# Two-block model on one core: the feed forward's single pair of inner rows moves from the first group of the product back to the last

## The chip, the cores and the metric

One core of a Trainium2 chip runs one program. The metric is the device time of that core in microseconds (us); less is better. The time before is the median of three runs.

## The reference, cut to what matters

Two models run one after the other on a sequence of 256 tokens with width 1024: a first block (two layers with three branches each), then a second block (two layers, each a mixing part and a feed forward). The second block also carries a context of 256 tokens. Its feed forward is what the change touches:

```python
D_FF = 2816
def conv_ffn(h, w_up, conv_w, w_down):
    a = dwconv_centred(h @ w_up, conv_w)      # three taps along the tokens
    val, gate = jnp.split(a, 2, axis=-1)
    return (val * jax.nn.silu(gate)) @ w_down

x = x + g2 * conv_ffn(hf, w_up[l], conv_w[l], w_down[l])
if not last:                                  # layer 0 does the context too
    xc = xc + cg2 * conv_ffn(hcf, w_up[l], conv_w[l], w_down[l])
```

In layer 0 both streams go through, 512 columns wide; in layer 1 only the 256 tokens. Behind it stands a root mean square norm with a scale and a shift that come from a conditioning vector (`c`, `c_ctx`) through `w_mod`.

## The kernel before, in words

Activations lie with their channels on the partitions: `t_X` holds 8 tiles of 128 channels by two streams of 256 tokens, all in float32. To keep that precision, every weight and every activation is split into a high and a low part, and each product is three matmuls: high by high, high by low, low by high (L1003, L1004, L1005 in `chan`).

**Weights.** They arrive in rows of 128 by 1024 floats, loaded by SP's queue into 8 raw buffers. A `split` step turns a row into a high part on ScalarE (L1410) and then a low part on VectorE (L1740). There are 5 slots (`NS`) for split chunks. The split of chunk i + 5 waits until TensorE has used chunk i for the last time (`used`), and it stands in the order of ScalarE and VectorE where the planner put it.

**The order.** One planner (`Order`) writes a single list of steps. Each engine goes through this list in order and does its own part of each step, with semaphore waits in between. `gemm` plans one product: it takes chunks of weights, cuts the output into parts that each take one of four PSUM banks (`gb0` to `gb3`, reused in turn), puts the split of the chunk five ahead of its first one before the last part, and that of its second chunk, if it has one, behind. `tick` lets generators in `self.side` add one step each (gated products, sums of squares). An `urgent` product (the last of a stage) cuts its last parts finer, ticks between the parts and leaves the splits of its own chunks to the norm behind it (`late`, `high_first`, `lows`, `late_splits`). `mod_turn` puts a conditioning step (`mod`, matmuls L1095) after every third product of the feed forward in layer 0, as long as more than 6 of them are left; its bank is emptied by `modsum` on VectorE (L1801) or, for every fourth one, on ScalarE (L1456).

**The feed forward of layer 0** (`block2(0)`). The 2816 inner rows are 22 tiles, handled as 11 pairs. For each pair there are two up products, value (`vg` = 0) and gate (`vg` = 1), each 8 tiles deep with 256 output rows: 48 matmuls of 512 columns. Behind each part ScalarE applies the middle tap (L1700) and VectorE the side taps (L2185, twice). `glu` follows one product later: SiLU on ScalarE (L1710), product on VectorE (L2200), high part on ScalarE (L1712), low part on VectorE (L2202), into `Y2` and `YL2`, which hold two groups of four tiles. The product back, `down(g)`, reads one group and comes in two halves of 512 output rows. Each half has four parts (m = 0 to 3), one bank each, and its two x updates per part are L2158 on VectorE. The groups are: pair 0 alone (two tiles), then pairs 1 and 2, 3 and 4, 5 and 6, 7 and 8, 9 and 10 (four tiles each). A half with two tiles takes one chunk of weights, a half with four tiles takes two.

`down(5)` ends the feed forward. Before it, the generator of the squares is put in `self.side`: squares of x tiles 0 to 3 behind the first half, 4, 5, 6 and 7 one by one behind the parts of the second half, which is urgent (`down`, c = 11). A square is L1436 on ScalarE and its sum L1765 on VectorE. Then the norm: TensorE's sum over the partitions in two steps (L1077, which waits for the sum with tile 6, and L1068), conditioning steps between them, the root on ScalarE, the reciprocal on VectorE, its spread over the partitions (L1084), the normalised tiles on VectorE and ScalarE (`norm2`), and then the `wide` product of layer 1, whose tiles are taken as the norm hands them over.

The lines that the steps speak of: the group of a pair is `g, p2 = (pr + 1) // 2, (pr + 1) % 2`, written out in `block2`, in `glu` on ScalarE and VectorE and in `ffup` on both. In `down` of TensorE, `yv` is the first slot of the group in `Y2`. The order of the up and down products:

```python
for vg in range(len(first), 2):
    self.gemm("up", ...)
if p2 == 1 and g >= 1:
    self.need_mods(l, 5)
    down(g - 1)
```

Of the kernel before, what the change touches and what calls it, by code (L numbers as in the profile page):

```python
# [66 lines left out]
class Marks:  # L67
# [17 lines left out]
    def at(self, *event):  # L85
        return self.table[event] if self.sems else {}
# [76 lines left out]
class Order:  # L163
# [427 lines left out]
    def block2(self, l):  # L591
        last = l == L - 1
        tw = 256 if last else 512
        nz = tw // 256
        t = 3 + 2 * l
        self.every = 0 if last else 3
        if last:
            self.need_mods(l, 1)
            self.add("s1", l=l, x=(1, t))
            b = self.rstd(t, (1, 1, 1))  # L600
            self.add("norm2", l=t, g=b, x=range(8))
            self.behind_sums()
            self.late_splits()
            self.wide(l, [("uf", c, wcols("w_in_2", l, 768 + np.arange(c * 256, c * 256 + 256)), 256, lambda m: (0, 1), None)
                          for c in range(2)], 256, t)
        else:
            self.between()
        self.side.append(self.mixes(l, nz))
        self.fine = True
        i = self.chunk(CH, wcols("w_in_2", l, np.concatenate([BY_HALF, 64 + BY_HALF, 128 + np.arange(128)])))  # L610
        self.add("k2", l=l, i=i, g=(self.bank(),))
        self.rope2_then(l, "k", 0)
        self.tick()
        self.split_after(i, 0)
        self.add("v2", l=l, i=i, g=(self.bank(),))
        self.side.append(self.v2_turn(l))
        self.split_after(i, 1)
        self.tick()
        for c in range(2):
            self.gemm("q2", l, c, wcols("w_in_2", l, 256 + LAT_PERM.reshape(8, 64)[4 * c:4 * c + 4, BY_HALF].reshape(256)), 8, 256, tw,  # L620
                      then=lambda m0: [self.rope2_then(l, "q", 2 * c + m) for m in range(m0, min(2, m0 + 512 // tw))] and ())
        self.drain()
        units = [(z, m, qb) for z in range(nz) for m in range(4) for qb in range(2)]
        self.side.append(self.staggered([self.pair(l, n, *u) for n, u in enumerate(units)], range(len(units))))
        for bi, nkt, wn, perm in ((1, 2, "w_br_pool_2", None), (2, 2, "w_br_four_2", None), (0, 4, "w_br_attn_2", LAT_PERM)):
            for c in range(4):
                self.gemm("gate2", l, c, wcols("w_in_2", l, 1280 + bi * 1024 + np.arange(c * 256, c * 256 + 256)), 8, 256,
                          tw, x=(bi, tw))
                if bi == 0 and c == 0:
                    self.drain()  # L630
                if bi == 0 and c == 3:
                    for k in range(6):
                        self.add("msplit2", l=l, c=k)
                self.gemm("proj2", l, c, wcols(wn, l, np.arange(c * 256, c * 256 + 256), perm), nkt, 256, tw,
                          x=(bi, tw, nkt, len(units)))
        self.fine = False
        for k in (6, 7):
            self.add("msplit2", l=l, c=k)
        self.tick()
        self.need_mods(l, 2)  # L640
        self.every = 0
        self.side.append(self.squares(t + 1, PAIRED))
        def wout2(c):
            return wcols("w_out_2", l, np.arange(c * 256, c * 256 + 256))
        first = (0, 1) if last else (0,)
        self.wide(l, [("wout2", c, wout2(c), 256, lambda m: (m, min(2, m + 512 // tw)), None) for c in first], tw, -1)
        for c in first:
            self.tick()
            self.mod_turn()
        for c in range(len(first), 4):  # L650
            self.gemm("wout2", l, c, wout2(c), 8, 256, tw, urgent=c == 3, early=last, soon=c == 2)
        self.drain()
        self.need_mods(l, 4)
        self.add("s1", l=l, x=(4, t + 1))
        b = self.rstd(t + 1, (1, 1, 1 if last else 2))
        self.add("norm2", l=t + 1, g=b, x=range(8))
        self.behind_sums()
        self.late_splits()
        self.every, self.keep = 0 if last else 3, 6

        def down(g):
            nt = 4 if g else 2
            for half in range(2):
                self.gemm("down", l, 2 * g + half, wcols("w_down_2", l, np.arange(half * 512, half * 512 + 512),
                                                         max(0, 4 * g - 2) * 128 + np.arange(nt * 128)), nt, 512, tw,
                          urgent=g == 5 and half == 1, early=not last, x=(nt,))
        for pr in range(11):
            g, p2 = (pr + 1) // 2, (pr + 1) % 2
            first = () if pr else range(512 // tw if last else 1)
            if pr == 0:  # L670
                self.wide(l, [("up", 0, wcols("w_up_2", l, vg * DFF + np.arange(256)), 256,
                               lambda m, vg=vg: (m, min(2, m + 512 // tw), vg),
                               lambda m, vg=vg: self.up_then(l, 0, vg, m, tw)) for vg in first], tw, t + 1)
                self.tick()
                self.mod_turn()
            for vg in range(len(first), 2):
                self.gemm("up", l, pr, wcols("w_up_2", l, vg * DFF + np.arange(pr * 256, pr * 256 + 256)), 8, 256, tw,
                          x=(vg,), then=lambda m0: self.up_then(l, pr, vg, m0, tw))
            if p2 == 1 and g >= 1:
                self.need_mods(l, 5)  # L680
                down(g - 1)
                if not last and g == 3:
                    self.add("c3", l=1)
        self.drain()
        self.side.append(self.squares(t + 2, ((0, 1, 2, 3), (4, 5), (6,), (7,)) if last else ((0, 1, 2, 3), (4,), (5,), (6,), (7,))))
        down(5)
        self.drain()
        self.every = 0
# [204 lines left out]


IDLE = {0: (11, 2, 5), 1: (0, 0, 1), 4: (0, 0, 1), 5: (0, 0, 3), 6: (0, 0, 2)}


def blocks_of(s):
# [68 lines left out]
def tensor(e, units, t, M):  # L967
# [53 lines left out]
    def idle(b, t_, part):  # L1021

        src = t.C32.rearrange("p k c -> p (k c)") if t_ == 0 and part == 0 else t.C1
        for _ in range(IDLE.get(t_, (0, 0, 0))[part]):
            mm(b[:, 0:256], src[:, 0:128], src[:, 0:256], start=True, stop=True)
# [327 lines left out]

    def down(u):
        tw, g, nt = 256 if u.l else 512, u.c // 2, u.x[2]
        yv = (g % 2) * 4 + 4 - nt
        chan(u, nt, 512, tw, lambda k: t.Y2[:, yv + k, 0:tw], lambda k: t.YL2[:, yv + k, 0:tw],
             lambda k: at("glu", u.l, g, yv + k), ("downmm", u.l, g))

# [27 lines left out]
def scalar(e, units, t, M):  # L1387
# [305 lines left out]

    def ffup(u):
        l, pr, vg, tw = u.l, u.c, u.x[2], 256 if u.l else 512
        D, p2 = (t.VT, t.GT)[vg], (pr + 1) % 2
        b = gbank(u)
        for j, m in enumerate(range(u.x[0], u.x[1])):
            q.wait_ge(was("fr", l, vg, pr - 2, m), at("m2", l))
            act(D[:, p2, m, 0:tw], b[:, j * tw:(j + 1) * tw], ACT.Copy,  # L1700
                scale=vec("conv2", (l * 3 + 1) * 44 + vg * 22 + 2 * pr + m)).then_inc(*up("act", ("upa", l, pr, vg, m)))

    def glu(u):
        l, pr, tw = u.l, u.c, 256 if u.l else 512
        g, p2 = (pr + 1) // 2, (pr + 1) % 2
        for m in range(u.x[0], u.x[1]):
            yi = (g % 2) * 4 + 2 * p2 + m
            G, V = t.GT[:, p2, m, 0:tw], t.VT[:, p2, m, 0:tw]
            q.wait_ge(at("upd", l, pr, 1, m))
            act(G, G, ACT.Silu).then_inc(*up("act", ("glus", l, pr, m)))  # L1710
            q.wait_ge(at("gluv", l, pr, m), was("downmm", l, g - 2), at("wout2mm", l))
            act(t.Y2[:, yi, 0:tw], V, ACT.Copy).then_inc(*up("act", ("gluh", l, pr, m), ("glu", l, g, yi), ("fr", l, 0, pr, m)))  # L1712
# [10 lines left out]
def vector(e, units, t, M):  # L1723
    q, up, at, was, last = Queue(e, M), M.up, M.at, M.was, lambda: M.last("dve")
# [449 lines left out]

    def ffup(u):
        l, pr, vg, tw = u.l, u.c, u.x[2], 256 if u.l else 512
        D, p2, b = (t.VT, t.GT)[vg], (pr + 1) % 2, t.gb[u.g[0] % 4]
        ms = list(enumerate(range(u.x[0], u.x[1])))

        def side(j, m, w):  # L2180
# [11 lines left out]

    def glu(u):
        l, pr, tw = u.l, u.c, 256 if u.l else 512
        g, p2 = (pr + 1) // 2, (pr + 1) % 2
        for m in range(u.x[0], u.x[1]):
            yi = (g % 2) * 4 + 2 * p2 + m
            G, V = t.GT[:, p2, m, 0:tw], t.VT[:, p2, m, 0:tw]
# [259 lines left out]
```

## Time and profile before

| What | Value |
|---|---|
| Median of 3 runs | 2054.66 us (2052.29 to 2056.34) |
| Profiled execution, its own time | 2052.45 us |
| Its span, first to last instruction | 2050.7 us |
| TensorE busy | 2030.4 us, 99% |
| VectorE busy | 1361.2 us, 66% |
| ScalarE busy | 1100.1 us, 54% |
| GpSimd busy | 71.3 us, 3% |
| Mean granted TensorE clock | 0.998 |
| Feed forward of layer 0 | about 1280 to 1650 us of the span |

The busy time of TensorE is modelled from pipelined matmuls: a record of 0.39 us stands every 0.23 us, so records overlap, and the distance of two starts tells the pace. An idle time is shown in brackets in front of the instruction that ended it, with the instruction that released it.

### The profile page before, as it was taken

What the parts mean: (1) busy time and instruction counts of PE and PEld (TensorE: products, weight loads), DVE (VectorE), ACT (ScalarE), POOL (GpSimd) and SP (SyncE); (2) the same over time, 40 slices, a digit from 0 to 9 for tenths busy, and PEclk for the clock granted to TensorE, in tenths of its full rate; (3) what the DMA queues carried; (4) which work ended last, traced back from release to release, by engine and by line L of the source; (5) the groups of instructions that cost most, each with busy time, mean ns of one, the idle gap of its engine ahead of it and who ended that gap; (6) DMA issues with size and microseconds to landing.
All of it is one profiled execution on the core that took longest, in us unless ns stands there. A gap on an engine that the chain in (4) does not pass through costs nothing.

```text
span 2050.7 us, 36323 instructions
## 1 busy us (share of the span) xinstructions
PE 2030.4 (99%) x14736; PEld 1822.3 (89%) x14736; DVE 1361.2 (66%) x2349; ACT 1100.1 (54%) x1839; POOL 71.3 (3%) x55
## 2 busy tenths in 40 slices
PE   9999999999999999999999999999999999999998
PEld 9999999999999999998777887778888878999998
DVE  6787767557687777574565345665555667668786
ACT  5576676545676685553575233433332357655554
POOL 1310000000300000000000000000000000000000
PEclk9999999999999999999999999999999999999999
DMA  8546645567656635563223434433343344456552
GB/s 296 184 159 215 191 145 166 194 210 253 225 171 198 205 124 190 201 206 134 90 73 114 144 134 144 145 114 131 113 159 123 104 154 131 147 178 217 186 181 67
DMA packets 97351, 333.97 MB, mean 163 GB/s; under 512 B 11552, under 2 KB 16160, under 8 KB 96928
## 3 DMA queue, kind: packets, MB, share of 16 engines
q1 hardware_dynamic: 97184, 331.64, 47.8%
q8 instruction: 117, 1.92, 0.4%
q14 instruction: 50, 0.41, 0.1%
HBM read 326.49 MB, written 1.18 MB: 160 GB/s over the span
## 4 chain that ended last, share of the span: by engine, by line
PE 92%; DVE 4%; ACT 2%; issue 1%; DMA 0%; DVEq 0%; SPq 0%; ACTq 0%
PE ps L1003 26%; PE ps L1004 25%; PE ps L1005 25%; PE ps L1095 2%; PE ps L1016 2%; PE ps L1017 1%; PE ps L1018 1%; PE ps L1315 1%; PE ps L1168 1%; DVE t_lo L1740 1%; PE ps L1336 1%; PE ps L1325 1%; PE ps L1184 1%; ACT t_hi L1410 1%; PE ps L1149 1%
## 5 line engine op out<-in xcount | busy, mean ns | idle before, releaser
L1003 PE MATMUL ps<-t_RB,t_hi 128*128 128x256 f32 (+1 forms) x3712 | 1160.2, 313 | 3.8 <-DVE t_MT L1801 2.2
L1004 PE MATMUL ps<-t_RB,t_hi 128*128 128x256 f32 (+1 forms) x3712 | 1144.0, 308 | 0.0
L1005 PE MATMUL ps<-t_RB,t_lo 128*128 128x256 f32 (+1 forms) x3712 | 1143.7, 308 | 0.0
L1740 DVE TENSOR_TENSOR t_lo<-t_raw,t_hi 128x1024 fp32r<-128x1024 f32 (+1 forms) x500 | 604.7, 1225 | 357.7 <-ACT t_hi L1410 356.2
L1003 PEld LDWEIGHTS ps<-t_RB,t_hi 128*128 128x128 f32 x3712 | 707.9, 191 | 72.4 <-issue 22.7
L1005 PEld LDWEIGHTS ps<-t_RB,t_lo 128*128 128x128 f32 x3712 | 708.1, 191 | 35.3
L1004 PEld LDWEIGHTS ps<-t_RB,t_hi 128*128 128x128 f32 x3712 | 708.4, 191 | 33.0
L1410 ACT ACTIVATE t_hi<-t_raw 128x1024 fp32r<-128x1024 f32 (+1 forms) x506 | 519.4, 1041 | 376.4 <-PE ps L1005 353.5
L2185 DVE SCALAR_TENSOR_TENSOR t_A<-ps,t_V,t_A 128x510 f32<-128x510 f32 (+1 forms) x176 | 102.1, 611 | 89.7 <-ACT t_A L1700 88.1
L1700 ACT ACTIVATE t_A<-ps,t_V 128x512 f32<-128x512 f32 (+1 forms) x88 | 48.4, 576 | 127.2 <-PE ps L1005 127.2
L2158 DVE SCALAR_TENSOR_TENSOR t_X<-ps,t_MOD,t_X 128x256 f32<-128x256 f32 x168 | 72.5, 477 | 33.1 <-PE ps L1005 33.1
L1016 PE MATMUL ps<-t_hi,t_RB 128*128 128x256 f32 x256 | 74.8, 292 | 0.0
L1017 PE MATMUL ps<-t_hi,t_RB 128*128 128x256 f32 x256 | 73.0, 285 | 0.0
L1018 PE MATMUL ps<-t_lo,t_RB 128*128 128x256 f32 x256 | 73.0, 285 | 0.0
L1686 ACT ACTIVATE t_A<-ps 128x512 f32<-128x512 f32 (+1 forms) x48 | 22.3, 490 | 84.3 <-PE ps L1005 84.3
L1712 ACT ACTIVATE t_RB<-t_A 128x512 fp32r<-128x512 f32 (+1 forms) x44 | 23.1, 526 | 57.5 <-DVE t_A L2200 57.5
L1016 PEld LDWEIGHTS ps<-t_hi,t_RB 128*128 128x128 f32 x256 | 49.7, 194 | 1.5 <-DVE t_RB L2047 0.5
L1095 PE MATMUL ps<-t_raw,t_C 128*32 128x256 f32 x768 | 51.0, 385 | 0.0
L1017 PEld LDWEIGHTS ps<-t_hi,t_RB 128*128 128x128 f32 x256 | 49.8, 195 | 0.0
L1018 PEld LDWEIGHTS ps<-t_lo,t_RB 128*128 128x128 f32 x256 | 49.7, 194 | 0.0
L1436 ACT ACTIVATE t_NT<-t_X 128x256 f32<-128x256 f32 (+1 forms) x56 | 24.8, 467 | 37.5 <-DVE t_X L2158 21.6
L1966 DVE SCALAR_TENSOR_TENSOR t_A<-ps,t_V,t_A 128x255 f32<-128x255 f32 (+2 forms) x96 | 41.7, 475 | 1.1
(307 smaller groups left out, 1846.2 us busy)
## 6 DMA issues: line engine op xcount, KB each, us to landing
t_raw<-in_W SPq DMA_DIRECT2D x586, 512.0 KB, 4.0
t_A<-cu_scratch SPq DMA_DIRECT2D x8, 512.0 KB, 6.1
t_B<-cu_scratch SPq DMA_DIRECT2D x8, 512.0 KB, 6.1
t_raw<-in_W SPq DMA_DIRECT2D x16, 256.0 KB, 2.8
t_A<-t_T SPq DMA_DIRECT2D x40, 64.0 KB, 4.5
t_A<-in_C SPq DMA_DIRECT2D x2, 1280.0 KB, 7.2
t_A<-t_T SPq DMA_DIRECT2D x40, 32.0 KB, 1.9
t_X<-in_X SPq DMA_DIRECT2D x2, 512.0 KB, 4.4
```

The source lines that it names most:

```text
L1003: mm(o, hi[:, w], xh(k), start=k == 0 and j == 0, stop=False)
L1004: mm(o, hi[:, w], xl(k), start=False, stop=False)
L1005: i = mm(o, lo[:, w], xh(k), start=False, stop=k == nkt - 1 and m == u.x[1] - 1)
L1016: mm(o, xh(k, tb), hi[:, w], start=k == 0 and j == 0, stop=False)
L1017: mm(o, xl(k, tb), hi[:, w], start=False, stop=False)
L1018: i = mm(o, xh(k, tb), lo[:, w], start=False, stop=k == nkt - 1 and tb == blocks[-1])
L1095: i = mm(b[32 * c:32 * c + 32, 0:256], t.C32[:, k, :], t.raw[r % NR][:, c * 256:c * 256 + 256], start=u.s[0] and h == 0, stop=u.s[1] and h ...
L1410: act(t.hi[s][:, 0:w], t.raw[r][:, 0:w], ACT.Copy).then_inc(*up("act", ("hi", u.i), ("split", u.i)))
L1700: act(D[:, p2, m, 0:tw], b[:, j * tw:(j + 1) * tw], ACT.Copy, scale=vec("conv2", (l * 3 + 1) * 44 + vg * 22 + 2 * pr + m)).then_inc(*up("a ...
L1740: tt(t.lo[s][:, 0:w], t.raw[r][:, 0:w], t.hi[s][:, 0:w].bitcast(F), ALU.subtract).then_inc(*up("dve", ("split", u.i)))
L2158: stt(out=x, in0=ps[:, z * 256:z * 256 + 256], scalar=t.modv(u.l, j, k, z), in1=x, op0=ALU.mult, op1=ALU.add).then_inc(*up("dve", ("x", s, ...
L2185: return stt(out=o[:, :, r], in0=ps[:, :, s], scalar=cw, in1=o[:, :, r], op0=ALU.mult, op1=ALU.add)
```

## The change

In layer 0 the pairs are grouped 0 and 1, 2 and 3, and so on to 8 and 9, and pair 10 is a group by itself. So the group with two tiles is the last one of the product back instead of the first. Layer 1 keeps the grouping that both had. A function `pair_of(l, pr)` gives group and place of a pair for both layers: `divmod(pr + l, 2)`. The products back of layer 0 then follow up 3, 5, 7, 9 and 10 (before: 2, 4, 6, 8 and 10), and `down(5)` comes last as before. The load of the constants `c3` follows `down(2)` in both.

```diff
         def down(g):
-            nt = 4 if g else 2
+            nt = 2 if g == (0 if last else 5) else 4
             for half in range(2):
                 self.gemm("down", l, 2 * g + half, wcols("w_down_2", l, np.arange(half * 512, half * 512 + 512),
-                                                         max(0, 4 * g - 2) * 128 + np.arange(nt * 128)), nt, 512, tw,
+                                                         (max(0, 4 * g - 2) if last else 4 * g) * 128 + np.arange(nt * 128)), nt, 512, tw,
                           urgent=g == 5 and half == 1, early=not last, x=(nt,))
         for pr in range(11):
-            g, p2 = (pr + 1) // 2, (pr + 1) % 2
+            g, p2 = pair_of(l, pr)
...
-            if p2 == 1 and g >= 1:
+            if (p2 == 1 or pr == 10) and g >= 1:
                 self.need_mods(l, 5)
                 down(g - 1)
...
+def pair_of(l, pr):
+
+    return divmod(pr + l, 2)
...
     def down(u):
         tw, g, nt = 256 if u.l else 512, u.c // 2, u.x[2]
-        yv = (g % 2) * 4 + 4 - nt
+        yv = (g % 2) * 4 + (4 - nt if g == 0 else 0)
...
     def ffup(u):
         l, pr, vg, tw = u.l, u.c, u.x[2], 256 if u.l else 512
-        D, p2 = (t.VT, t.GT)[vg], (pr + 1) % 2
+        D, p2 = (t.VT, t.GT)[vg], pair_of(l, pr)[1]
...
     def glu(u):
         l, pr, tw = u.l, u.c, 256 if u.l else 512
-        g, p2 = (pr + 1) // 2, (pr + 1) % 2
+        g, p2 = pair_of(l, pr)
```

`ffup` and `glu` change in the same way on ScalarE and on VectorE.

## Rows read from the trace of the kernel before

**Rows 1.** The page: the engines' busy time, the chain that ended last.
```profile
PE 2030.4 (99%) x14736; PEld 1822.3 (89%) x14736; DVE 1361.2 (66%) x2349; ACT 1100.1 (54%) x1839; POOL 71.3 (3%) x55
PE 92%; DVE 4%; ACT 2%; issue 1%; DMA 0%; DVEq 0%; SPq 0%; ACTq 0%
```

**Rows 2.** Waits of PE, 1250 to 1720 us: total us, times, longest; both that there are.
```profile
PE ps L1003 <- DVE t_MT L1801: 2.2, 1, 2.2
PE ps L1077 <- DVE t_SQA L1765: 1.2, 1, 1.2
```

**Rows 3.** Timeline of PE in the first product back: start us, duration us, instruction, [idle].
```profile
1353.30 0.39 PE L1005 MATMUL ps<-t_RB,t_lo 128*128 128x512 f32 x1
1355.91 0.50 PE L1003 MATMUL ps<-t_RB,t_hi 128*128 128x512 f32 x1 [2.22 <-DVE t_MT L1801]
```

**Rows 4.** Timeline of DVE at the same place.
```profile
1351.46 0.68 DVE L2200 TENSOR_TENSOR t_A<-t_A 128x512 f32<-128x512 f32 x1
...
1355.44 0.41 DVE L1801 TENSOR_TENSOR t_MT<-t_MT,ps 128x256 f32<-128x256 f32 x1
1355.77 2.44 DVE L2158 SCALAR_TENSOR_TENSOR t_X<-ps,t_MOD,t_X 128x256 f32<-128x256 f32 x6
```

**Rows 5.** Timeline of PE: ends of down 5's halves, and the norm behind.
```profile
1638.52 0.39 PE L1005 MATMUL ps<-t_RB,t_lo 128*128 128x512 f32 x1
...
1649.39 0.39 PE L1005 MATMUL ps<-t_RB,t_lo 128*128 128x512 f32 x1
1650.95 1.02 PE L1077 MATMUL ps<-t_C,t_SQA 128*128 128x1 f32 x8 [1.17 <-DVE t_SQA L1765]
...
1654.89 0.65 PE L1084 MATMUL ps<-t_C,t_SM 128*128 128x128 f32 x4
```

**Rows 6.** Timeline of DVE in down 5.
```profile
1636.22 0.88 DVE L2158 SCALAR_TENSOR_TENSOR t_X<-ps,t_MOD,t_X 128x256 f32<-128x256 f32 x2 [1.84 <-PE ps L1005]
1638.73 1.23 DVE L1740 TENSOR_TENSOR t_lo<-t_raw,t_hi 128x1024 fp32r<-128x1024 f32 x1 [1.63 <-ACT t_hi L1410]
1639.88 0.87 DVE L2158 SCALAR_TENSOR_TENSOR t_X<-ps,t_MOD,t_X 128x256 f32<-128x256 f32 x2
1640.66 2.27 DVE L1765 TENSOR_TENSOR t_SQA<-t_SQA,t_NT 128x512 f32<-128x512 f32 x3
1642.99 1.23 DVE L1740 TENSOR_TENSOR t_lo<-t_raw,t_hi 128x1024 fp32r<-128x1024 f32 x1
1644.13 0.87 DVE L2158 SCALAR_TENSOR_TENSOR t_X<-ps,t_MOD,t_X 128x256 f32<-128x256 f32 x2
...
1646.37 0.87 DVE L2158 SCALAR_TENSOR_TENSOR t_X<-ps,t_MOD,t_X 128x256 f32<-128x256 f32 x2
```

**Rows 7.** Timeline of ACT: the high part in the first half of down 5.
```profile
1637.64 1.06 ACT L1410 ACTIVATE t_hi<-t_raw 128x1024 fp32r<-128x1024 f32 x1 [8.46 <-PE ps L1005]
```

**Rows 8.** Windows: stretch, us, busy us (x) of PE to POOL, PEclk, DMA share, GB/s.
```profile
921.00:924.00 3.00, 1.85 (x24) 1.39 (x24) 1.02 (x4) 1.49 (x4) 0.00 (x0) 1.00 0.12 49
924.00:928.00 4.00, 4.00 (x24) 3.89 (x21) 3.57 (x9) 1.93 (x4) 0.00 (x0) 0.57 0.72 262
...
1638.90:1650.00 11.10, 10.88 (x49) 8.67 (x47) 8.80 (x15) 6.24 (x11) 0.00 (x0) 1.00 0.28 94
...
1654.00:1657.00 3.00, 3.00 (x38) 1.62 (x37) 2.02 (x6) 1.17 (x4) 0.00 (x0) 1.00 1.00 340
```

**Rows 9.** Timeline of PE around 924 us, where the second block begins.
```profile
918.06 0.28 PE L1018 MATMUL ps<-t_lo,t_RB 128*128 128x256 f32 x1
918.18 0.28 PE L1016 MATMUL ps<-t_hi,t_RB 128*128 128x256 f32 x1
...
922.15 0.58 PE L1077 MATMUL ps<-t_C,t_SQA 128*128 128x1 f32 x4 [1.29 <-DVE t_SQA L1765]
...
925.02 0.41 PE L1016 MATMUL ps<-t_hi,t_RB 128*128 128x256 f32 x1
925.24 0.41 PE L1017 MATMUL ps<-t_hi,t_RB 128*128 128x256 f32 x1
```

More of the change, by code:

```diff
@@ L2176, in ffup @@
         l, pr, vg, tw = u.l, u.c, u.x[2], 256 if u.l else 512
-        D, p2, b = (t.VT, t.GT)[vg], (pr + 1) % 2, t.gb[u.g[0] % 4]
+        D, p2, b = (t.VT, t.GT)[vg], pair_of(l, pr)[1], t.gb[u.g[0] % 4]
         ms = list(enumerate(range(u.x[0], u.x[1])))
@@ L2194, in glu @@
         l, pr, tw = u.l, u.c, 256 if u.l else 512
-        g, p2 = (pr + 1) // 2, (pr + 1) % 2
+        g, p2 = pair_of(l, pr)
         for m in range(u.x[0], u.x[1]):
```

## The prediction

> **What bounds the kernel now.** The page comes first. TensorE is busy for 99% of the span and the chain that ended last lies on it for 92% [rows 1], so the change can only act where TensorE stands still, or where it runs at another clock. The work of the product is the same in both kernels: 22 up products, and 22 tiles of inner rows for the product back, however they are grouped. So the next view is the list of TensorE's own waits in the stretch of this feed forward (1250 to 1720 us). It holds two entries: 2.2 us, once, for the sum L1801 into t_MT, and 1.2 us, once, for the sum of squares L1765 [rows 2]. The first lies at the small group that now stands at the start, the second right behind the last group. Both are touched by the change, in opposite directions.
>
> The profiled execution took 2052.45 us (span 2050.7, the rest lies around it). The median of the three runs is 2054.66, 2.2 above it. My sum is a difference, worked out in the profiled execution and added to the median.
>
> **The start stall goes: -2.4 us.** Matmuls of 512 columns follow each other every 0.2265 us (48 matmuls from 1638.52 to 1649.39 [rows 5]). A quarter (one m) of a half of down has 3 matmuls per tile: 12 with four tiles, 2.72 us, and 6 with two tiles, 1.36 us. In the small group at the start, down c=1 takes its fourth bank back from the conditioning matmuls issued between its two halves. That bank is freed by the VectorE sum L1801, which is queued behind the two gated products of pair 2 (1351.46 to 1355.4) [rows 4]. TensorE gets to the point after three quarters of 1.36 us and stops: it issues at 1353.30 and next at 1355.91, where 1353.53 was due: 2.38 lost [rows 3]. After the change the first group has four tiles, and counting the chunks' products (one conditioning step per three) its step comes behind up 3's value half, followed by the gate half (48 matmuls, 10.9 us) before the bank comes round again. L1801 is 4 us late at most, so 10.9 us cover it. The next step comes behind down c=1, again before an up product. Value -2.4; bounds 0 (another bank takes its place) and -2.6 (with the slow first matmuls after the stall).
>
> **Order inside the body: 0.** Every down product has the same two up products between it and the last gated product that it reads, except the last pairs. Down 4 reads pair 9, with down 3's second half and up 10 in between (over 30 us); down 5 reads pair 10, with the 21.7 us of down 4 (96 matmuls) in between, as now. The buffers Y2/YL2 are freed one product before they are written, as now. If that cover were gone, a wait for a gated product would cost about the 4 us of its chain [rows 4]. The c3 load and the weight loads keep their order in SP's queue. c3 is issued one pair (about 22 us) later, but its reader is in the next layer; 0. The conditioning steps are as many as before. Split steps: as many, but one moves from behind the norm to before it (below).
>
> **The end: +5.7 us.** This is the term that decides. Call E0 the end of the first half of down 5 (1638.91: last issue 1638.52 plus 0.39) and E the end of its last matmul (1649.78) [rows 5]. Between them TensorE now has 10.87 us of work; with two tiles it has 5.44.
> VectorE's work there does not shrink. Now [rows 6]: low part of a chunk at 1638.73, the fourth x update at 1639.88 (E0+0.97), three sums of squares from 1640.66 (2.33 until the next), a low part at 1642.99 (1.14), the first x update of the last half at 1644.13. From there each quarter is a chain of x update, square on ScalarE and sum on VectorE, 2.2 us each (1644.13, 1646.37), whatever TensorE does. TensorE's sum over partitions starts when the seventh sum is done, at 1650.95, 6.82 behind that first update: E0+12.04, E+1.17.
> After: the low part of the chunk five ahead sits before the fourth x update in VectorE's order. The slot that it needs is now freed by the very last matmul of the half, since the chunk is the whole half, instead of by its sixth (1637.54, ScalarE's high part at 1637.64 [rows 7]). So the high part starts at E0+0.10, the low part at E0+1.19, the update at E0+2.34 (+1.15), the sums at E0+3.12 (+0.78), and the first update of the last half at E0+5.45 (+2.33; the second low part is gone, which saves 1.14). TensorE starts again at E0+5.45+6.82 = E0+12.27. But E is now E0+5.44. The gap is 6.83 instead of 1.17: +5.66.
> VectorE has idle time in the first half (1.84 before 1636.22 [rows 6]), but its next work there waits for TensorE, so none of it can be drawn ahead. Bounds: with no backlog at all the four-quarter chain alone, started at E-4.08, ends at E+2.8: +1.7; with a low part more in front, +6.8. I take 5.66, since each step has its own row. Nothing hides it: the conditioning matmuls put there to fill the norm stand behind the waiting instruction in TensorE's queue.
> Behind the norm one low part fewer waits. TensorE stood still for none there [rows 2], so that is 0.
>
> **The clock: +2.5 us.** The kernel's granted clock fell to half (1.2 of 2.4 GHz) only once before its end: at 924.3, after 1.29 us without work and thin work behind it (922.15 on) [rows 8, 9]. The distance of two matmuls went from 0.12 (918.06, 918.18) to 0.21 (925.02, 925.24). The 4 us from 924 have a mean clock of 0.57, so some 3.4 us ran at half, which cost 1.5. At the end of this feed forward, a gap of 1.17 left it at 1.00 [rows 5, 8]. A gap of 6.8 has no row; it is five times the one that was followed by a fall, so I take it that it falls. What follows the gap is a chain on TensorE: sum over partitions, conditioning step, second sum, conditioning step, spread of the root, 1650.95 to 1655.5, 4.5 us [rows 5]. At half clock it is longer by 0.78 (0.2133 against 0.12): 3.5 if the whole chain runs so, 1.5 if only as long a stretch does as at 924. Value 2.5. Bounds: 0, and 4.8 with some 1.3 more in the first steps of the wide product, which go at VectorE's pace.
> The Trainium skill (TensorE: Matmul & The Clock Gate, the part on the HAM clock gate) says that an idle stretch puts the engine back to 1.2 GHz and that only sustained work brings it back. It speaks against this change: by it the fall is certain and the sum +5.8. By the gap that left the clock at 1.00 alone, the sum would be +3.3. The trace agrees that the clock can fall within the kernel, not yet how surely.
>
> **Sum.** -2.38 + 5.66 + 2.5 = +5.8: the profiled execution would come to 2058.2, the median to 2060.4. A measurement of this kernel tells about 0.2% (4.1 us) from no change.
>
> **The rivals.**
> (a) The clock holds. For: 1.17 us did nothing. Against: the gap is almost six times that. -2.4 + 5.7 = +3.3: 2058.0, within 0.2%. Chance 0.15.
> (b) The other side: VectorE keeps up, and only the start stall's removal is left. Place: first update of the last half. For: there is room, since VectorE is busy for 8.8 of 11.1 us of the last half as it is [rows 8], and a low part leaves its queue. The change comes out not slower if the gap behind E is under 1.17 + 2.4 = 3.6 us, that is if that update starts by E0+2.2 instead of E0+5.45. Against: low part, update and three sums, 4.3 us, stand before it in order. Full case: 2052.3; at its border 2054.7. Chance 0.12.
> (c) The start stall returns at another bank or gated product: +8.2, 2062.8. Against: products of 10.9 us instead of 5.4 everywhere. Chance 0.08.
> (d) The clock stays low through the chain and into the wide product, since thin work does not raise it: -2.4 + 5.7 + 4.8 = +8.1: 2062.7. For: thin work at 921 to 924 was followed by the fall [rows 8]. Chance 0.14.
> (e) The change does nothing, since the group sizes are the same set: 2054.7; it would need both gaps unchanged. Chance 0.02.
> My forecast has the remaining 0.49.
>
> **How the numbers follow.** The likeliest is 2060.4. Its own spread is about 2 either way (clock term 1.5 to 3.5, median of a few runs about 1). The range takes in (a), (c), (d) and the forecast: 2056.2 to 2064.4, and leaves out (b), (e) and tails. Slower by over 0.2% (above 2058.8): most of the forecast (0.42) and (c), (d): 0.64. Within 0.2%: (a), (e), most of (b) (0.10) and the low part of the forecast (0.07): 0.34. Faster by over 0.2% (below 2050.6) needs more than the 3.6 us of both stalls together, so it is left with 0.02 out of (b).
>
> **What would show it.** In the profile after: no wait of L1003 for L1801 near 1354; TensorE idle 6 to 7 us before L1077 at some 1648 to 1654, released by L1765; 24 matmuls of L1003 to L1005 between the two halves' ends; the x update, square, sum rhythm of 2.2 us unchanged; a clock under 1.00 in the windows behind the gap, matmul records there longer by about three quarters; the later stages shifted as a whole. It is wrong if the gap is under 3.6 us, or if a new wait shows in the body.

## The result, and the profile after

The changed kernel takes 2058.70 us in the median of 16 runs (2057.72 to 2059.68). The kernel before, in 16 runs beside it and before it, takes 2055.97 (2052.29 to 2057.52). The ratio is 1.0019, with a 95% interval of 1.0012 to 1.0025: slower by 2.5 to 5.1 us, just inside the 0.2% that the prediction had set as its line. The predicted median was 2060.4 in a range of 2056.2 to 2064.4, with 0.64 on slower by over 0.2%, which did not come, and 0.34 on a difference within it.

The profiled execution took 2058.21 us with a span of 2056.4; the prediction had 2058.2 for it.

| | before | after |
|---|---|---|
| Median, 16 runs each | 2055.97 us | 2058.70 us |
| Profiled execution / span | 2052.45 / 2050.7 us | 2058.21 / 2056.4 us |
| Mean granted clock of it | 0.998 | 0.995 |
| TensorE's waits, 1250 to 1720 us | 2.2 and 1.2 us | 6.7 us |
| From the sum over partitions to the spread of the root | 4.6 us | 8.4 us |

The page after, the lines that answer to [rows 1] (busy time; chain that ended last):

```profile
PE 2033.1 (99%) x14736; PEld 1823.9 (89%) x14736; DVE 1360.7 (66%) x2349; ACT 1100.7 (54%) x1839; POOL 71.4 (3%) x55
...
PE 93%; DVE 4%; ACT 2%; issue 1%; DVEq 0%; ACTq 0%
```

As many matmuls as before, and the busy share still reads 99%. These two lines would not lead anyone to the cause. The list of PE's waits from 1250 to 1720 us does. It has one entry (lines have moved by 5; L1082 is the sum over the partitions, L1770 the sum of squares):

```profile
PE ps L1082 <- DVE t_SQA L1770: 6.7, 1, 6.7
```

The start wait of [rows 2] is gone and the one at the end has grown from 1.2 to 6.7 us. PE's timeline there, to be held beside [rows 5]:

```profile
1640.10 0.39 PE L1010 MATMUL ps<-t_RB,t_lo 128*128 128x512 f32 x1
...
1645.54 0.39 PE L1010 MATMUL ps<-t_RB,t_lo 128*128 128x512 f32 x1
1652.62 1.84 PE L1082 MATMUL ps<-t_C,t_SQA 128*128 128x1 f32 x8 [6.68 <-DVE t_SQA L1770]
1654.38 1.93 PE L1100 MATMUL ps<-t_raw,t_C 128*32 128x256 f32 x16
1656.24 1.87 PE L1073 MATMUL ps<-t_C,t_NT 128*128 128x1 f32 x8
1658.04 1.93 PE L1100 MATMUL ps<-t_raw,t_C 128*32 128x256 f32 x16
1659.91 1.12 PE L1089 MATMUL ps<-t_C,t_SM 128*128 128x128 f32 x4
```

1640.10 is the last matmul of the first half, 1645.54 that of the second, 24 matmuls later. Behind the gap every record takes 1.7 to 1.8 times as long as in [rows 5]: 1.84 for 1.02 us, 1.12 for 0.65. The windows show why (columns as in [rows 8]):

```profile
924.00:928.00 4.00, 4.00 (x40) 3.75 (x33) 3.42 (x9) 1.93 (x4) 0.00 (x0) 1.00 0.74 262
1646.00:1652.00 6.00, 0.00 (x0) 0.00 (x0) 3.85 (x9) 3.62 (x6) 0.00 (x0) 0.77 0.00 0
1652.00:1656.00 4.00, 3.38 (x24) 2.37 (x24) 2.65 (x6) 1.32 (x2) 0.00 (x0) 0.50 0.12 16
1656.00:1662.00 6.00, 6.00 (x44) 3.68 (x44) 1.54 (x5) 0.69 (x3) 0.00 (x0) 0.50 0.91 336
1662.00:1666.00 4.00, 4.00 (x33) 3.04 (x23) 4.00 (x11) 2.68 (x8) 0.00 (x0) 0.89 0.89 329
```

The clock falls within the gap and stays at half (1.2 of 2.4 GHz) through the whole thin chain, until the wide product is about to begin. At 924, where the profiled execution before had lost 1.5 us, the clock holds this time. VectorE's and ScalarE's timelines for the same place, beside [rows 6, 7]:

```profile
1640.59 1.06 ACT L1415 ACTIVATE t_hi<-t_raw 128x1024 fp32r<-128x1024 f32 x1 [4.38 <-PE ps L1010]
```

```profile
1641.68 1.23 DVE L1745 TENSOR_TENSOR t_lo<-t_raw,t_hi 128x1024 fp32r<-128x1024 f32 x1 [1.31 <-ACT t_hi L1415]
1642.82 0.87 DVE L2163 SCALAR_TENSOR_TENSOR t_X<-ps,t_MOD,t_X 128x256 f32<-128x256 f32 x2
1643.61 2.28 DVE L1770 TENSOR_TENSOR t_SQA<-t_SQA,t_NT 128x512 f32<-128x512 f32 x3
1645.80 0.87 DVE L2163 SCALAR_TENSOR_TENSOR t_X<-ps,t_MOD,t_X 128x256 f32<-128x256 f32 x2
1647.43 0.69 DVE L1770 TENSOR_TENSOR t_SQA<-t_SQA,t_NT 128x512 f32<-128x512 f32 x1 [0.76 <-ACT t_NT L1441]
1648.04 0.87 DVE L2163 SCALAR_TENSOR_TENSOR t_X<-ps,t_MOD,t_X 128x256 f32<-128x256 f32 x2
```

When the first update of the last half starts (1645.80), TensorE has already issued that half's last matmul (1645.54).

Where 5.5 of the 5.8 us between the two profiled executions come from: the last matmul of down 5 ends at 1645.93 instead of 1649.78 (-3.85: the start stall of 2.4, and the fall at 924 that is absent here, 1.5). The gap is 6.68 instead of 1.17 (+5.51). From its end to the end of the spread it takes 8.41 instead of 4.59 (+3.82). Together +5.48; the first matmul behind the wide product starts at 1676.06 instead of 1670.58, also 5.48 later. The wide product itself starts 5.96 later (1664.04 instead of 1658.08): the half clock also cost 0.5 us in the steps between the spread and the wide product, and the wide product made that up.

### The profile page after: what moved, and what is told of

Same layout as the page of the kernel before. It is cut to its first block, busy times and chain, and to the rows that moved or that the text cites. A ratio compares the mean times of both kernels' runs of the same rounds, so it can differ in the third digit from the quotient of the medians.

```text
span 2056.4 us, 36322 instructions
## 1 busy us (share of the span) xinstructions
PE 2033.1 (99%) x14736; PEld 1823.9 (89%) x14736; DVE 1360.7 (66%) x2349; ACT 1100.7 (54%) x1839; POOL 71.4 (3%) x55
## 4 chain that ended last, share of the span: by engine, by line
PE 93%; DVE 4%; ACT 2%; issue 1%; DVEq 0%; ACTq 0%
PE ps L1008 26%; PE ps L1009 25%; PE ps L1010 25%; PE ps L1100 2%; PE ps L1021 1%; PE ps L1022 1%; PE ps L1023 1%; PE ps L1320 1%; PE ps L1173 1%; DVE t_lo L1745 1%; PE ps L1341 1%; PE ps L1330 1%; PE ps L1189 1%; PE ps L1154 1%; PE ps L1030 1%
```

## The experiments

Theory T is the prediction's: two gaps of TensorE, both made by VectorE's queue, and the clock behind the one at the end. Theory U: the clock falls in any case in the thin work of the norm (its small matmuls, of one column or on 32 columns of weights), and the gap hardly matters. Theory V: the regrouping costs time in the body of the loop. Each ratio is to the kernel before on the same chip, with its 95% interval. In diffs, `A` stands for the changed kernel as base and `B` for the kernel before.

| Kernel | Median us (runs) | Kernel before beside it | Ratio | Span of its profile |
|---|---|---|---|---|
| mid_pair | 2054.04 (12) | 2055.38 | 0.9996 (0.9988 to 1.0005) | 2049.3 |
| before_turn | 2055.87 (12) | 2055.38 | 1.0001 (0.9993 to 1.0010) | 2054.2 |
| before_fill | 2053.05 (12) | 2055.38 | 0.9993 (0.9984 to 1.0001) | 2052.7 |
| after_fill | 2059.62 (11) | 2055.38 | 1.0018 (1.0010 to 1.0027) | 2056.3 |
| after_fill13 | 2055.49 (11) | 2054.51 | 1.0005 (0.9996 to 1.0014) | 2053.6 |
| after_late | 2055.81 (11) | 2054.51 | 1.0009 (1.0000 to 1.0018) | 2056.0 |
| before_glu | 2051.09 (11) | 2054.51 | 0.9987 (0.9978 to 0.9996) | 2050.7 |
| glu_pipe | 2047.08 (5) | 2054.51 | 0.9967 (0.9954 to 0.9979) | 2045.2 |
| after_pipe | 2057.54 (11) | 2056.16 | 1.0010 (1.0001 to 1.0019) | 2055.8 |
| before_pipe | 2052.36 (11) | 2056.16 | 0.9984 (0.9975 to 0.9993) | 2050.6 |
| after_all | 2051.11 (11) | 2056.16 | 0.9977 (0.9968 to 0.9986) | 2049.7 |
| glu_pipe_fill | 2049.51 (6) | 2056.16 | 0.9969 (0.9958 to 0.9981) | 2046.4 |

### The start: which part of the small group makes the wait

**mid_pair**: pair 4 alone, so that first and last group both have four tiles.

```diff
 def pair_of(l, pr):
-    return divmod(pr + l, 2)
+    return divmod(pr + (l or pr > 4), 2)
...
-            nt = 2 if g == (0 if last else 5) else 4
+            nt = 2 if g == (0 if last else 2) else 4
-            if (p2 == 1 or pr == 10) and g >= 1:
+            if (p2 == 1 or (pr == 4 and not last)) and g >= 1:
```

The row offset follows, and `VT`, `GT` go by `pr % 2`.

> The pair of two tiles stands in the middle (pair 4 is a group by itself), so both the first and the last group have four tiles. Theory T (two gaps): the start wait of 2.2 us is gone, the gap behind down 5 is back at 1.2 us, the chain of the norm takes 4.6 us at full clock in most executions; profiled span 2048.3 (2050.7 less 2.4), median 2 to 3 us under the kernel before and 4 to 8 us under the changed one. Theory V (the regrouping itself costs time in the body of the loop): a wait of 1 us or more shows somewhere between 1290 and 1630, and the time is not under that of the kernel before.

The end came out as T had it: the gap is 1.17 us again. The start did not: T had the wait gone. It has moved with the small group (PE's timeline):

```profile
1490.33 0.50 PE L1008 MATMUL ps<-t_RB,t_hi 128*128 128x512 f32 x1 [2.22 <-DVE t_MT L1806]
```

It is as long as in [rows 3] and stands at down 2, now the small one. The span of 2049.3 is 1.4 under the kernel before because the clock held at 924 in this execution; the ratio shows no difference from 1, where T had the median 2 to 3 us lower. Theory V falls as well: the list of waits from 1250 to 1720 has these two entries and no other.

**before_turn**: the conditioning steps moved by one product, so that none stands between the halves of the small group.

```diff
         self.every, self.keep = 0 if last else 3, 6
+        self.turn += 0 if last else 1
```

> The kernel before with the conditioning steps of this feed forward moved by one product, so that none stands between the halves of the small group. Groups as before. Theory T: only the start wait goes, 2.2 to 2.4 us less (span 2048.3), the gap at the end stays at 1.2. If the wait at the start was the small group's own (shorter parts against VectorE's queue, whoever holds the bank), a wait of 1 to 2 us stays there and the gain is under 1 us.

The second case came true, with a longer wait than the 1 to 2 us expected. It has another releaser, the x update instead of the conditioning sum:

```profile
1355.23 0.50 PE L1004 MATMUL ps<-t_RB,t_hi 128*128 128x512 f32 x1 [2.58 <-DVE t_X L2159]
```

So the bank's holder was not the cause. VectorE is busy with the two gated products from 1350.33 to 1354.3 here too, and whatever frees a bank stands behind them.

This profile shows something else that the prediction had at nothing. Right behind the stall the clock falls. The windows there (columns as in [rows 8]), before_turn first, then before_fill (see below; its stall is 2.22 us, as in [rows 3]), then the kernel before:

```profile
1356.00:1360.00 4.00, 4.00 (x12) 3.09 (x11) 2.66 (x5) 0.00 (x0) 0.00 (x0) 0.58 0.28 81
```

```profile
1356.00:1360.00 4.00, 4.00 (x11) 3.15 (x12) 2.56 (x7) 1.06 (x1) 0.00 (x0) 0.57 0.06 23
```

```profile
1356.00:1360.00 4.00, 4.00 (x18) 3.29 (x19) 3.45 (x8) 1.06 (x1) 0.00 (x0) 1.00 0.08 28
```

While it is down the 512-column matmuls start 0.43 us apart instead of 0.23, and the fall costs 1.6 us each time. It shows in three of the five profiles that have such a stall (before_turn, before_fill, before_pipe; not in the kernel before nor in mid_pair) and in none of the nine that have no such stall, the changed kernel's among them. So where the clock falls the start stall costs 4.0 us and not 2.4.

**before_glu**: the gated product of pair 2 one product later, the conditioning step where it was.

```diff
-    def later(self, kind, **k):
+    def later(self, kind, more=0, **k):
         def g():
             yield
+            for _ in range(more):
+                yield
...
-            self.later("glu", l=l, c=pr, x=
+            self.later("glu", more=int(l == 0 and pr == 2), l=l, c=pr, x=
```

> The kernel before with the gated product of pair 2 one product later, behind the second half of the small group instead of between its halves. The conditioning step stays between the halves. mid_pair and before_turn have shown that the start wait follows the small group whoever holds the bank; theory T now says that it is the 4 us of gated product in VectorE's queue ahead of the first half's last x update. Expected: no wait at 1354, 2.2 to 2.4 less; span 2048.3 where the clock holds, median 2 us under the kernel before. If the small group's parts are too short for VectorE even without it, a wait of 0.5 us or more stays.

The wait is gone; only the end's is left in the list of PE's waits, and the conditioning sum (now L1803) runs at 1352.16 instead of 1355.44 ([rows 4]), right behind the x update:

```profile
1351.38 0.87 DVE L2160 SCALAR_TENSOR_TENSOR t_X<-ps,t_MOD,t_X 128x256 f32<-128x256 f32 x2
1352.16 0.41 DVE L1803 TENSOR_TENSOR t_MT<-t_MT,ps 128x256 f32<-128x256 f32 x1
```

The ratio of 0.9987 (2.7 us, interval 0.8 to 4.5) agrees with 2.4 us, and with some more. In its profile the sum over the partitions starts 1.82 us earlier than in [rows 5] (1649.13 against 1650.95); the execution was already 0.7 us late at 922. One thing stays open: T had 2048.3 for the span of an execution in which the clock holds, and none of the 11 came to that (the lowest took 2050.50, the mean clock was 0.996 or 0.997 in all). So the start stall is made by short parts and the gated products together: 5.4 us of matmuls per half against 4 us of VectorE that nothing may pass.

### The clock behind the last group

**after_fill** and **after_fill13** (A), **before_fill** (B): matmuls without use in TensorE's queue ahead of the sum over the partitions, 24, 13 and 4 of them. `u.l == 5` is the norm behind this feed forward.

```diff
     def rstda(u):
...
         b = bank(u)
+        for _ in range(13 if u.l == 5 else 0):
+            mm(b[:, 0:256], t.C1[:, 0:128], t.C1[:, 0:256], start=True, stop=True)
         q.wait_ge(at("sqadd", u.l, 6))
```

> The changed kernel with 24 matmuls of 256 columns (float32, 0.26 us each, 6.3 us) that compute nothing of use, in TensorE's queue between the last matmul of down 5 and the sum over the partitions. They add no wait: the sum's wait for L1770 still ends last. Theory T: the gap of 6.7 is filled, the clock stays at 1.00, the chain from the sum to the spread of the root takes 4.6 us instead of 8.4; span 2052.6 or so, 3.5 to 4 us under the changed kernel. Theory U (the clock falls by itself in the thin work of the norm, gap or no gap): the clock still shows under 1 behind 1652 and the time stays within 1 us of the changed kernel. If the gap is not VectorE's doing, the fillers push the sum back and the time rises by up to 6 us.

The price per filler was wrong: each leaves two records, 0.22 us apart, so 24 took 10.6 us and pushed the sum back by 4.2 us (1656.86 instead of 1652.62). That mistake makes it a clean measurement of the clock. PE's timeline:

```profile
1646.40 10.63 PE L1081 MATMUL ps<-t_C 128*128 128x256 f32 x48 [0.79 <-DVE t_X L2165]
1656.86 0.95 PE L1084 MATMUL ps<-t_C,t_SQA 128*128 128x1 f32 x8
...
1660.72 0.65 PE L1091 MATMUL ps<-t_C,t_SM 128*128 128x128 f32 x4
```

The chain starts 4.24 us later than in the changed kernel and ends at 1661.37, only 0.34 later, since it runs at full clock: 4.51 us against 8.41. The spans are 2056.3 and 2056.4.

> As after_fill, but 13 matmuls instead of 24: after_fill's record shows two passes of 0.22 us for each, so 24 took 10.6 us and outlasted the gap, while the chain behind them ran at full clock in 4.5 us. 13 take 5.7 us and end with the gap. Theory T: the sum starts when the seventh sum of squares is done, as in the changed kernel, the chain takes 4.6 us instead of 8.4: span 2052.6, median 3 to 4 us under the changed kernel's 2058.7, that is within 1.5 us of the kernel before. Theory U: clock under 1 there all the same, time as the changed kernel's.

```profile
1647.99 5.88 PE L1081 MATMUL ps<-t_C 128*128 128x256 f32 x26 [0.79 <-DVE t_X L2165]
1653.79 1.05 PE L1084 MATMUL ps<-t_C,t_SQA 128*128 128x1 f32 x8
...
1657.75 0.65 PE L1091 MATMUL ps<-t_C,t_SM 128*128 128x128 f32 x4
```

Here the last matmul of down 5 ends at 1647.20 (1647.99 less 0.79; this execution had lost time at 924, as the kernel before did). 6.6 us later the sum starts, the stretch being as long as before but full except for the first 0.79 us, and 4.6 us after that the chain is through. The ratio goes from the changed kernel's 1.0019 to 1.0005, and the median from 2058.7 to 2055.5 (on different chips). That is about 3 us; T had 3 to 4, and the intervals of the ratios are too wide to tell more. Theory U falls: with the gap filled the clock holds through the thin chain. All 14 profiles, the kernels below included, bear this out. With the gap filled, gone, or 0.55 us long the clock held through the chain in seven of seven (after_fill, after_fill13, before_fill, after_all, before_pipe, glu_pipe, glu_pipe_fill). Behind 4.4 to 6.7 us it was at half in three of three (the changed kernel, after_late, after_pipe). Behind 1.17 us it held in two (the kernel before, mid_pair) and fell in two (before_turn, before_glu).

> The kernel before with 4 such matmuls (1.0 us) in its gap of 1.2 us. Theory T: same span as the kernel before when that one keeps its clock (2050.7); if the other executions of the kernel before (median 3.5 us above the profiled one) lose time by a fall of the clock behind this gap, the median falls by 1 to 3 us. Theory U: no change of the median, since the thin work behind is what counts.

The median beside its own kernel before is 2.3 us lower (2053.05 against 2055.38), as T had it, with an interval of the ratio that just includes 1. These fillers were too many as well: they took 1.7 us in a gap of 1.17 and pushed the sum back by 0.55 us. The clock held behind them in the profile. This fits the wider scatter of the kernel before, which the falls at 1356 add to. In the 90 executions of the kernel before that stand beside these experiments, 26 took under 2054 us, with a mean clock of 0.997 to 0.998; the others, up to 2058.9, show 0.994 to 0.997. The changed kernel always shows 0.994 to 0.996. before_glu's profile, with the kernel before's gap of 1.17, shows such an execution:

```profile
1649.13 1.02 PE L1079 MATMUL ps<-t_C,t_SQA 128*128 128x1 f32 x8 [1.17 <-DVE t_SQA L1767]
1650.08 1.07 PE L1097 MATMUL ps<-t_raw,t_C 128*32 128x256 f32 x16
1651.08 1.33 PE L1070 MATMUL ps<-t_C,t_NT 128*128 128x1 f32 x8
1652.34 1.93 PE L1097 MATMUL ps<-t_raw,t_C 128*32 128x256 f32 x16
1654.20 1.12 PE L1086 MATMUL ps<-t_C,t_SM 128*128 128x128 f32 x4
```

The clock falls in the middle of the chain (the third record is 1.33, the fourth 1.93 instead of 1.07). The end of the spread is at 1655.32, 0.2 us before that of [rows 5], although the chain began 1.8 us earlier.

### The end: what makes the gap

**after_late** (A): the split of the first half's chunk leaves the half and joins those behind the norm.

```diff
             if last and not urgent and hold:
+                self.late.append(i)
+            elif last and not urgent:
                 self.split_after(i, 0)
```

`hold` is set for the first half of down 5 in layer 0.

> The changed kernel, with the split of the chunk that the first half of down 5 frees moved out of the half (as the last half's already is): its high part comes behind the last part, its low part behind the sum over the partitions. Theory T (VectorE's queue sets the gap): the fourth x update starts at E0+0.1 to 0.2 instead of E0+2.3, so the gap shrinks by 2.2, from 6.7 to 4.5; the chain is at half clock as before; span 2 us under the changed kernel's. If the gap were the four-quarter chain's alone, it would stay at 6.7.

VectorE's fourth x update comes right behind TensorE, and the gap shrinks to 4.40 us, by 2.28:

```profile
1642.87 0.88 DVE L2165 SCALAR_TENSOR_TENSOR t_X<-ps,t_MOD,t_X 128x256 f32<-128x256 f32 x2 [0.15 <-PE ps L1012]
```

```profile
1652.67 0.56 PE L1084 MATMUL ps<-t_C,t_SQA 128*128 128x1 f32 x2 [4.40 <-DVE t_SQA L1772]
```

The gap is as expected. The span of its profile is not 2 us lower, since this execution was 0.8 us later at 922 already, then had a fall at 924 (1.5 us), and so came to the end of down 5 2.3 us later than the changed kernel's. The ratio, 1.0009 against 1.0019, agrees with 2 us, with overlapping intervals.

**after_pipe** (A), **before_pipe** (B), **glu_pipe** (before_glu and this edit): each sum of squares one part later, so that VectorE never waits for a square that ScalarE has only just begun.

```diff
-((0, 1, 2, 3), (4,), (5,), (6,), (7,))
+((0, 1, 2), (3,), (4,), (5, 6), (7,))
```

> The changed kernel with the sums of squares one part later in VectorE's order, as in glu_pipe. Theory T: the split ahead of the fourth x update stays, the chain of update, square, sum no longer costs 2.2 us a part; first update of the last half at E0+4.6 instead of 5.5, seventh sum done at E0+10.5: gap 5.0 instead of 6.7, clock still half behind it, span and median 1.5 to 2 us under the changed kernel. If the gap were set by the amount of VectorE's work alone and not by the order, it would stay at 6.7.

The gap is 5.09 us. The parts are now 1.4 us apart on VectorE (1646.48 and 1647.87 instead of 2.2 apart), about what TensorE needs for one part of the short half (1.36):

```profile
1646.48 0.87 DVE L2163 SCALAR_TENSOR_TENSOR t_X<-ps,t_MOD,t_X 128x256 f32<-128x256 f32 x2
1647.27 0.68 DVE L1770 TENSOR_TENSOR t_SQA<-t_SQA,t_NT 128x512 f32<-128x512 f32 x1
1647.87 0.87 DVE L2163 SCALAR_TENSOR_TENSOR t_X<-ps,t_MOD,t_X 128x256 f32<-128x256 f32 x2
```

The same VectorE work in another order gave 1.6 us of gap back. So it is the order, not the amount alone. What is left of the gap comes from two things. The low part, one update and two sums still stand in front of the last half's first update, which starts 4.5 us behind the first half's end. And the seventh sum waits for ScalarE, whose square for it stands behind the loading of a table (VectorE's timeline, then ScalarE's):

```profile
1651.65 0.69 DVE L1770 TENSOR_TENSOR t_SQA<-t_SQA,t_NT 128x512 f32<-128x512 f32 x1 [0.94 <-ACT t_NT L1441]
```

```profile
1649.47 1.28 ACT L1427 ACT_TABLE_LOAD   x1
1650.77 0.20 ACT L1427 ACTIVATE t_INI<-t_V 64x1 f32<-64x1 f32 x1
1650.99 0.63 ACT L1441 ACTIVATE t_NT<-t_X 128x512 f32<-128x512 f32 x1
```

The update that this square reads ended at 1650.1, so some 0.9 us of this gap are the table's. after_all has the same wait of 0.94 us. No run moved the load.

> The kernel before with the sums of squares one part later, nothing else. Theory T: the start wait of 2.2 stays, the gap at the end goes (0.4 or less) and with it most falls of the clock: best execution 1.2 us under the best of the kernel before, median 3 to 5 us under its median. Were the falls due to the thin work of the norm alone, the median would come down by the 1.2 only.

No wait is left at the end of the kernel before. The median beside it falls by 3.8 us (2052.36 against 2056.16). The gap itself was 1.2, so the rest should be falls of the clock that no longer come; by the ratio the gain is 3.3 us (interval 1.4 to 5.1), so this rest is only just clear of the noise. The start stall and its fall at 1356 are still there in its profile. The best execution is 2050.78 against 2052.16, 1.4 less.

> before_glu, and the sums of squares at the end one part later in VectorE's order: x update, then the sum of the tile before, so that VectorE no longer waits for ScalarE's square in every part (the sums with tiles 5 and 6 come together before the last update). Theory T: the gap of 1.2 behind down 5 goes to 0.4 or less, the clock falls there in fewer executions; span 2047.5, median 3 to 5 us under the kernel before.

Both repairs together: between 1250 and 1720 us the list of TensorE's waits is empty.

```profile
1642.96 0.88 DVE L2160 SCALAR_TENSOR_TENSOR t_X<-ps,t_MOD,t_X 128x256 f32<-128x256 f32 x2 [1.06 <-PE ps L1007]
```

```profile
1645.49 0.98 PE L1079 MATMUL ps<-t_C,t_SQA 128*128 128x1 f32 x8
```

VectorE waits for TensorE in the last half (1.06 us), and the sum over the partitions starts without a gap, 5.46 us before that of [rows 5]. The ratio of 0.9967 means 6.8 us less than the kernel before (interval 4.3 to 9.5). It beats both kernels, though in 5 runs only.

**after_all** is A with after_late, after_pipe and 5 fillers; **glu_pipe_fill** is glu_pipe with 2 fillers.

> The changed kernel with both repairs of VectorE's order (after_late and after_pipe) and 5 idle matmuls (2.2 us) in the gap. Theory T: seventh sum at E0+7.7, gap 2.3 and filled, clock at 1.00 in most executions; median 2050 to 2052, under both kernels, and 2 to 4 us above glu_pipe's 2047.1: a short last half still costs time against a long one.

> glu_pipe with 2 idle matmuls (0.9 us) ahead of the sum over the partitions, where nothing waits any more. Theory T: 0.5 to 0.9 us slower than glu_pipe, since TensorE has no gap left there, with the same clock.

after_all is faster than both original kernels too, 0.9977: with VectorE's order mended, a small last group no longer costs much. A gap of 0.55 us is left behind the fillers, which the table's loading on ScalarE makes. The comparison with the long last group stays open: glu_pipe_fill has 0.9969 beside it, with overlapping intervals. Whether the fillers cost glu_pipe its expected 0.5 to 0.9 us cannot be told either, since the ratios are 0.9967 and 0.9969; the spans of the profiles are 2045.2 and 2046.4, 1.2 apart.

## Why the prediction was right, and where a term was off

**The start stall, -2.4.** Right for the profiled execution: no wait stands there after. For the median it was too small, since in part of the executions the clock falls behind the stall, for 1.6 us more, and the prediction had no term for that. The cause given for it was half right. The prediction named the conditioning sum's bank and its place behind the gated products. before_turn took the bank's holder away and the wait stayed; before_glu took the gated products away and it went. Rival (c) did not come: products of 10.9 us hide 4 us of VectorE. mid_pair shows that the stall returns wherever a small group meets a gated product.

**Order inside the body, 0.** Right: no wait between 1280 and 1640 us.

**The end, +5.7.** Right by its own steps. With E0 at 1640.49, the high part starts at E0+0.10 (predicted 0.10), the low part at 1.19 (1.19), the update at 2.33 (2.34), the sums at 3.12 (3.12), the first update of the last half at 5.31 (5.45), TensorE at 12.13 (12.27). The gap is 6.68 for 6.83, the term +5.51 for +5.66. (The lower bound of the step should read 1.6 and not 1.7: E-4.08 plus 6.82 is E+2.74.) after_late and after_pipe each removed one of its pieces and got 2.3 and 1.6 us back. Rival (b), that VectorE keeps up, needed the first update at E0+2.2.

**The clock, +2.5.** The direction was right: the gap of 6.7 was followed by a fall. By the Trainium skill's rule (TensorE: Matmul & The Clock Gate, the part on the HAM clock gate) it had to be, and the trace agrees: rival (a) fell. The size was off: the whole chain ran at half clock, +3.8, where the step took a middle between 1.5 and 3.5. Rival (d) came true for the chain, but the wide product ended no later for it. In the profiled pair this is made up for by the fall at 924, which only the execution before had (-1.5): -2.4 + 5.5 + 3.8 - 1.5 = +5.4, against +5.8 predicted. That the profiled execution came out at 2058.21 where 2058.2 was forecast is therefore luck: the clock term was 1.3 too small, and a fall that has nothing to do with the change took 1.5 off.

**The step that failed is the transfer to the median.** The prediction worked out its difference against the profiled execution of the kernel before and added it to the median of the runs. That execution held its clock both behind the start stall and behind the gap of 1.17 us. Profiles of kernels that share the stall or the gap show otherwise: behind the stall the clock falls in three of five (1.6 us each), behind the gap of 1.17 in two of four (before_turn, before_glu). Executions of the kernel before in which it falls already pay a part of the +3.8, and the change frees them of 4.0 us at the start instead of 2.4. The changed kernel has no stall at the start, and all its 16 runs show a mean clock of 0.994 to 0.996: it scatters by 2 us where the kernel before scatters by 5 to 7. The fall at 924 is no part of the difference: it stands in seven of the 14 profiles, of both kinds. Without it the profiled pair would differ by some 7 us. The medians differ by 2.7 and the ratio by 3.9 us instead of the 5.8 forecast. How often each fall comes in runs without a profile is not shown, only that the sizes fit. The sign held, the range held, and the 0.2% line was just not passed. The table of [rows 8] had 1.00 behind the gap, and the prediction took that one window for the rule, although the median of the runs, 2.2 us above the profiled execution, was a sign that other executions lose time somewhere.

## What to carry to other kernels

When a product's last part gets shorter, cost the engine that empties its banks in its own queue order: what stands there in front of the last part does not shrink with it. Here a stall of TensorE could cost twice, once as a stall and once more by the clock behind it (5.5 and 3.8 us at the end, 2.4 and in some executions 1.6 at the start). Matmuls without use in the gap gave back what the clock cost (after_fill13); a better order on VectorE gave back the stall too (before_pipe, glu_pipe). A difference worked out on one profiled execution holds for the median only if both kernels meet the clock in the same way; look at the scatter of the runs first.

## What was not expected of the hardware

The same gap of 1.17 us, with the same chain behind it, leaves the clock in one execution ([rows 8], 1.00) and is followed by a fall in another (before_glu, 1.33 and 1.93 us for records of 1.05 and 1.07). The stall of 2.2 to 2.6 us at the start has 512-column matmuls in front and behind, and the clock still fell behind it in three of five profiles. At 924 us, where the code is the same in all kernels, seven of the 14 profiles show a fall (0.57 in the kernel before) and seven do not (1.00 in the changed kernel).

How long the clock stayed down differed. At 924 and 1356 the mean over 4 us was about 0.6 and full clock was back behind it (1.00 from 1360 on in before_turn). Behind the gap of 6.7 us it stayed at 0.50 from 1652 to 1662 in the changed kernel, with conditioning matmuls and weight loads in all of it, and the chain took 1.83 times as long (8.41 against 4.59 us). In before_turn it was back within the conditioning step behind the spread, whose record of 1.34 us lies between 1.07 and 1.93.
